# Gates of 128 tokens put by indirect 4-byte DMAs, one-hots made in two VectorE operations, in a decoder block with a product-key expert layer

## What is computed

```python
q = (xt @ wq).reshape(t, PEER_HEADS, 2, PEER_HALF_DIM)          # 8 heads, 2 halves
sc = jnp.einsum('thpc,hpnc->thpn', q, sub_keys)                  # 128 keys a half
top_v, top_i = lax.top_k(sc, PEER_TOPK)                          # 16 of each half
cand_v = top_v[..., 0, :, None] + top_v[..., 1, None, :]         # 256 candidate pairs
best_v, best_pos = lax.top_k(cand_v, PEER_TOPK)                  # 16 experts a head
expert = take(top_i[0] * 128 + top_i[1], best_pos)               # of 128 * 128
gate = jax.nn.softmax(best_v, axis=-1)
hc = jnp.einsum('cd,chkd->chk', xc, u[ec])
ac = gate * jax.nn.gelu(hc)
out = jnp.einsum('chk,chkd->cd', ac, v[ec])
```

## Time and profile before

| | before |
|---|---|
| median of 3 runs | 3343.63 us (3340.43 to 3347.16) |
| the profiled execution | 3340.54 us, span 3338.7 us |
| busy, share of the span: PE | 3216.9 us, 96% |
| PEld | 2994.6 us, 90% |
| DVE | 2480.9 us, 74% |
| ACT | 1111.0 us, 33% |
| POOL | 535.9 us, 16% |

### The profile page before, as it was taken

The page is one execution under the profiler, slowest core; times in us unless marked ns, Lnnn a source line. Parts: engine busy times, 40 slices in busy tenths (PEclk is TensorE's granted clock), DMA queues, the critical chain, the costliest instruction groups (busy, mean ns, idle before and its releaser), DMA issues.

```text
span 3338.7 us, 48188 instructions
## 1 busy us (share of the span) xinstructions
PE 3216.9 (96%) x17333; PEld 2994.6 (90%) x17333; DVE 2480.9 (74%) x3744; ACT 1111.0 (33%) x1411; POOL 535.9 (16%) x381
## 2 busy tenths in 40 slices
PE   7999999999988889999999999999999999999997
PEld 5777788898888779999999999999999999999785
DVE  6444434699979977878888887888888888885644
ACT  4224423222225543333333323333233333333432
POOL 2120000011143221111212111121211112110200
PEclk8999999999999999999999999999999999999998
DMA  3231122333356667878878787887878878773222
GB/s 139 86 126 47 54 88 96 110 110 110 110 184 223 236 242 269 295 281 285 300 274 298 270 293 281 283 302 266 298 273 286 291 278 303 272 250 120 97 93 101
DMA packets 230385, 694.37 MB, mean 208 GB/s; under 512 B 17328, under 2 KB 75184, under 8 KB 194864
## 3 DMA queue, kind: packets, MB, share of 16 engines
q1 hardware_dynamic: 188848, 418.77, 36.5%
q0 software_dynamic: 36864, 268.45, 22.6%
q10 hardware_dynamic: 4608, 6.29, 0.5%
HBM read 657.79 MB, written 35.65 MB: 208 GB/s over the span
## 4 chain that ended last, share of the span: by engine, by line
PE 62%; issue 18%; DVE 12%; DMA 5%; ACT 2%; POOL 1%; DVEq 1%; SPq 0%; POOLq 0%; ACTq 0%
PE bank L475 19%; PE bank L476 19%; PE bank L477 19%; DVE one_g L1521 3%; DMA raw<-in_u_t 3%; DVE w_lo L1191 2%; DMA raw<-in_v 1%; DVE row L1497 1%; ACT w_hi L865 1%; POOL picked L1755 1%; PE bank L567 1%; PE bank L568 1%; PE bank L590 1%; DVE one_j L1524 1%; DVE x_lo L1629 1%
## 5 line engine op out<-in xcount | busy, mean ns | idle before, releaser
L475 PE MATMUL bank<-x_hi,w_hi 128*128 128x384 f32 (+1 forms) x3024 | 1081.9, 358 | 36.2 <-DVE x_lo L1208 16.1
L476 PE MATMUL bank<-x_lo,w_hi 128*128 128x384 f32 (+1 forms) x3024 | 1070.3, 354 | 0.0
L477 PE MATMUL bank<-x_hi,w_lo 128*128 128x384 f32 (+1 forms) x3024 | 1070.1, 354 | 0.0
L865 ACT ACTIVATE w_hi<-raw 128x1024 fp32r<-128x1024 f32 (+1 forms) x668 | 689.2, 1049 | 909.0 <-DMA raw<-in_v 336.2
L1191 DVE TENSOR_TENSOR w_lo<-raw,w_hi 128x1024 fp32r<-128x1024 f32 (+1 forms) x638 | 766.5, 1218 | 201.7 <-ACT w_hi L865 192.6
L475 PE MATMUL bank<-a_hi,w_hi 128*128 128x384 f32 x2048 | 688.1, 336 | 14.3 <-DVE w_lo L1191 10.9
L476 PE MATMUL bank<-a_lo,w_hi 128*128 128x384 f32 x2048 | 685.7, 335 | 0.0
L477 PE MATMUL bank<-a_hi,w_lo 128*128 128x384 f32 x2048 | 685.6, 335 | 0.0
L475 PEld LDWEIGHTS bank<-x_hi,w_hi 128*128 128x128 f32 x3024 | 571.7, 189 | 87.1 <-DVE w_lo L1191 21.9
L477 PEld LDWEIGHTS bank<-x_hi,w_lo 128*128 128x128 f32 x3024 | 571.4, 189 | 39.2
L476 PEld LDWEIGHTS bank<-x_lo,w_hi 128*128 128x128 f32 x3024 | 572.0, 189 | 38.6 <-issue 1.2
(11 more groups left out here) (194 smaller groups left out, 2183.0 us busy)
## 6 DMA issues: line engine op xcount, KB each, us to landing
raw<-in_u_t SPq DMA_DIRECT2D x256, 512.0 KB
raw<-in_v SPq DMA_DIRECT2D x256, 512.0 KB
gate_matrix<-g_blk SPq DMA_DIRECT2D x12, 2048.0 KB, 10.7
g_tile<-gate_matrix SPq DMA_DIRECT2D x32, 768.0 KB, 10.5
raw<-in_w_o SPq DMA_DIRECT2D x32, 512.0 KB
raw<-in_w_q SPq DMA_DIRECT2D x32, 512.0 KB
raw<-in_w_gate SPq DMA_DIRECT2D x32, 512.0 KB
raw<-in_w_in SPq DMA_DIRECT2D x26, 512.0 KB
```

What stands on the lines that cost most here:

```text
L475: pe.matmul(out, w_hi[slot][:, blk, :], m_hi, start=first, stop=False)
L476: pe.matmul(out, w_hi[slot][:, blk, :], m_lo, start=False, stop=False)
L477: return pe.matmul(out, w_lo[slot][:, blk, :], m_hi, start=False, stop=last)
L865: act.activation(w_hi[slot][:, 8 * s:8 * s + n, :], raw[s][:, 0:n, :], ACT.Copy)\
```

## The change

The tokens whose gates go through one-hots are the last 256 of the 384; blocks of one-hots fall from 12 to 8 (ONE_TB). The gates of the first 128 tokens (PUT_TB = 4 blocks) are written directly into `gate_matrix` in DRAM: SP first stores zeros there during the attention heads (from `zeros`, which lies where `x_rows` is later), VectorE computes for each head the flat position `cell` and the value `put_gate`, and GpSimd issues one indirect DMA for each (head, k) that adds 128 elements of four bytes, one for each token. One head's puts wait until those of the head before have landed. ScalarE waits for all puts ahead of the first block, SP ahead of the first gate load.

The `picked` product moves from GpSimd to VectorE, and `expert` is computed head by head; `topk_step` counts 22. The plain spilled units rise from 7 to 11 and get all their `w_lo` on VectorE; the first five of those splits stand within and right behind the last head's top-k. The sixteen early row dots are now eight ahead of the blocks and eight within. In `one_hots` the keys i and j are compared in one operation into `one_ij`, and a second one multiplies the i part by the gate into `one_g`.

The diff, cut to its core:

```diff
-ALONE = 7
-ALONE_POOL = 3
+ALONE = 11
+PUT_TB = P // TB
+ONE_TB = N_TB - PUT_TB
-EARLY = ALONE - ALONE_POOL + N_TB
+EARLY = 16
...
@@ SP @@
-            with sp.Fori(2, HEADS) as n:
+            sp.wait_ge(zeros_made, 1)
+            for n in range(2, HEADS):
                 load_unit(n + U_HEAD, head_w(n))
+                if n - 2 < 2 * PUT_TB:
+                    b, half = divmod(n - 2, 2)
+                    sp.dma_start(g_dram[b, :, 64 * half:64 * half + 64, :],
+                                 zeros[:, :].rearrange("p (i t) -> p i t", t=TB)).then_inc(zeros_stored, 16)
...
+            sp.wait_ge(gates_put, 16 * TOPK * PH)
             sp.wait_ge(spill_stored, 16 * N_GROUPS)
...
@@ TensorE @@
-            for e in range(1, ALONE_POOL + 1):
+            for e in range(1, 6):
                 alone(e)
...
-                for t in range(TCD):
+                for t in range(1, TCD):
                     mm = pe.transpose(bank[i][:, t * P:(t + 1) * P],
...
-            for e in range(ALONE_POOL + 1, ALONE):
+            for e in range(6, ALONE):
                 alone(e)
...
@@ ScalarE @@
-                if e == ALONE_POOL - 1:
+                if e == 3:
                     gates(PH - 1)
                 spill(2 * (PH - 1) + e, e % 2, U_ALONE + e)
-                if e == ALONE_POOL:
+                if e == 5:
...
+            act.wait_ge(gates_put, 16 * TOPK * PH)
             for s in range(2):
                 g_block(s, s)
...
@@ VectorE, keys_and_gates @@
+                dve.wait_ge(pick_ready, 2 * hd + 2)
+                for p in range(2):
+                    ins = dve.tensor_tensor(
+                        picked[p][:, :, :].rearrange("p (t k) m -> p t k m", t=TC),
+                        pick[p][:, :, :].rearrange("p (t k) m -> p t k m", t=TC),
+                        t_if[p][:, :, :].unsqueeze(2).to_broadcast([P, TC, TOPK, TOPK]), ALU.mult)
+                step(ins)
...
+                dve.tensor_tensor(of_head(put_gate), b_exp[:, 0, :], b_inv[:, 0:1].to_broadcast([P, TOPK]), ALU.mult)
...
-                dve.wait_ge(picked_ready, 2 * hd + 2)
...
+                dve.scalar_tensor_tensor(of_head(expert), i_of[:, TCD, :], float(NK), j_of[:, TCD, :], ALU.mult, ALU.add)
+                dve.scalar_tensor_tensor(pair_e[:, 0, :], j_of[:, 0, :], float(NK * TB),
+                                         rope_c[:, 2:3].to_broadcast([P, TOPK]), ALU.mult, ALU.add)
+                step(dve.tensor_scalar(pair_e[:, 1, :], i_of[:, 0, :], float(TB), None, ALU.mult))
+                step(dve.tensor_tensor(of_head(cell), pair_e[:, 0, :], pair_e[:, 1, :], ALU.add))
...
@@ VectorE, the last head, the row dots and the one-hots @@
+            lo(U_ALONE + 1, (U_ALONE + 1) % 2)
             half_topk(step, 2 * PH - 2, 0)
+            lo(U_ALONE + 2, U_ALONE % 2)
             half_topk(step, 2 * PH - 1, 1)
+            lo(U_ALONE + 3, (U_ALONE + 1) % 2)
             best_pairs(step)
+            lo(U_ALONE + 4, U_ALONE % 2)
             keys_and_gates(step, PH - 1)
...
+            lo(U_ALONE + 5, (U_ALONE + 1) % 2)
...
+            for k in range(ALONE - 5):
+                lo(U_ALONE + 6 + k, (U_ALONE + k) % 2)
                 row_dot(k, k % 2, row_loads(k))
-            row_dot(3, 1, row_loads(3))
+            for k in range(ALONE - 5, EARLY - ONE_TB):
+                row_dot(k, k % 2, row_loads(k))
...
-                for t in range(OH):
-                    ins = dve.tensor_scalar(one_g[s][:, t, :], iota[:, :], column(hk_t[0], q * OH + t),
-                                            column(hk_t[2], q * OH + t), ALU.is_equal, ALU.mult)
-                ins.then_inc(oh_g, 1)
-                dve.tensor_tensor(one_j[s][:, :, :], iota[:, None, :].to_broadcast(o),
-                                  hk_t[1][:, bass.ds(OH * q, OH)].unsqueeze(2).to_broadcast(o), ALU.is_equal)\
-                   .then_inc(oh_j, 1)
+                dve.tensor_tensor(one_ij[s][:, :, :, :], iota[:, None, None, :].to_broadcast(o),
+                                  hk_t[:, 0:2, bass.ds(OH * q + P, OH)].unsqueeze(3).to_broadcast(o), ALU.is_equal)\
+                   .then_inc(oh_ij, 1)
+                dve.wait_ge(oh_ij, q + 1)
+                dve.tensor_tensor(one_g[s][:, :, :], one_ij[s][:, 0, :, :],
+                                  hk_t[:, 2, bass.ds(OH * q + P, OH)].unsqueeze(2).to_broadcast([P, OH, NK]), ALU.mult)\
+                   .then_inc(oh_g, 1)
...
@@ GpSimd @@
+            pool.memset(zeros[:, :], 0.0).then_inc(zeros_made, 1)
...
+            def put_gates(hd, rows=None):
+
+                pool.wait_ge(topk_step, PER_TOPK * (hd + 1))
+                if hd:
+                    pool.wait_ge(gates_put, 16 * TOPK * hd)
+                for k in range(TOPK):
+                    if rows is not None and k % 4 == 0 and k:
+                        load_row(rows + k // 4 - 1)
+                    pool.indirect_dma_start(g_dram.rearrange("b j i t -> (b j i t)").unsqueeze(1),
+                                            bass.IndirectOffsetOnAxis(ap=cell[:, hd, k:k + 1], axis=0),
+                                            put_gate[:, hd, k:k + 1], None, compute_op=ALU.add)\
+                        .then_inc(gates_put, 16)
...
+            pool.wait_ge(zeros_stored, 16 * 2 * PUT_TB)
+            for hd in range(PH - 1):
+                put_gates(hd)
+            pool.wait_ge(topk_step, PER_TOPK * PH)
+            pool.wait_ge(rows_out, 4)
+            for k in range(2):
+                load_row(k)
+            put_gates(PH - 1, rows=2)
+            for k in range(5, EARLY - ONE_TB + 1):
+                load_row(k)
+            for b in range(ONE_TB):
+                if b and b + EARLY - ONE_TB < EARLY:
+                    load_row(b + EARLY - ONE_TB)
                 block_lo(U_BLOCK + 1 + b)
```

More of the change, by code:

```diff
@@ L119, in build_block @@
         x_rows = at("x_rows", rest + 7 * K, [P, D])
-        expert = at("expert", rest + 15 * K, [P, ROWS], U32)
+        zeros = x_rows
+        expert = at("expert", rest + 15 * K, [P, PH, TOPK], U32)
         gate_rows = at("gate_rows", rest + 15 * K + 512, [P, ROWS])
@@ L161, in build_block @@
         sel = [at(f"sel{i}", one + (42 + 2 * i) * K, [P, TC, PH, TOPK]) for i in range(3)]
+        pair_e = at("pair_e", one + 59 * K, [P, 2, TOPK])
+        cell = at("cell", one + 59 * K + 512, [P, PH, TOPK], U32)
+        put_gate = at("put_gate", one + 60 * K, [P, PH, TOPK])
         t_v = [at(f"t_v{i}", one + 48 * K + 256 * i, [P, TC, TOPK]) for i in range(2)]
@@ L170, in build_block @@
         t_if = [at(f"t_if{i}", one + 53 * K + 256 * i, [P, TC, TOPK]) for i in range(2)]
-        hk_t = [at(f"hk_t{i}", one + 2 * K * i, [P, TD]) for i in range(3)]
-        one_g = [at(f"one_g{i}", one + (14 + 4 * i) * K, [P, OH, NK]) for i in range(2)]
-        one_j = [at(f"one_j{i}", one + (22 + 4 * i) * K, [P, OH, NK]) for i in range(2)]
+        hk_t = at("hk_t", one, [P, 3, TD])
+        one_ij = [at(f"one_ij{i}", one + (6 + 8 * i) * K, [P, 2, OH, NK]) for i in range(2)]
+        one_g = [at(f"one_g{i}", one + (22 + 4 * i) * K, [P, OH, NK]) for i in range(2)]
         g_blk = [at(f"g_blk{i}", one + (30 + 16 * i) * K, [P, NK, TB]) for i in range(2)]
@@ L755, in g_group @@
                         o = 4 * half + t
-                        mm = pe.matmul(out[:, t * P:(t + 1) * P], one_j[s][:, o, :], one_g[s][:, o, :],
+                        mm = pe.matmul(out[:, t * P:(t + 1) * P], one_ij[s][:, 1, o, :], one_g[s][:, o, :],
                                        start=True, stop=True)
@@ L1785, in load_row @@
                 pool.indirect_dma_start(row[b][:, :], None, u_rows if k < ROWS else v,
-                                        bass.IndirectOffsetOnAxis(ap=expert[:, k % ROWS:k % ROWS + 1], axis=0))\
+                                        bass.IndirectOffsetOnAxis(ap=expert[:, k % ROWS // TOPK, k % TOPK:k % TOPK + 1], axis=0))\
                     .then_inc(row_in[b], 16)
-            pool.wait_ge(expert_ready, 1)
-            pool.wait_ge(rows_out, 4)
-            for k in range(6):
-                load_row(k)
             def block_lo(u):
@@ L1800, in block_lo @@
                         .then_inc(lo_ready, 1)
[L1802 to L1804 removed]
+            pool.wait_ge(zeros_stored, 16 * 2 * PUT_TB)
[11 more added lines that the diff above has]
+                    load_row(b + EARLY - ONE_TB)
                 block_lo(U_BLOCK + 1 + b)
             for s in range(2):
[L1807 removed]
+                pool.wait_ge(g_stored[s], 16 * (ONE_TB // 2))
             for k in range(EARLY, 2 * ROWS):
```

95 lines of the change are left out of this document (35 added, 60 removed).

## The result

The kernel after takes 3308.11 us (median; 3305.56 to 3311.9), the kernel before, run beside it, 3345.39 us (3340.43 to 3348.09): a ratio of 0.9893, with a 95% interval from 0.9878 to 0.9908. The profiled executions have spans of 3338.7 and 3308.0 us, 30.7 apart.

A forecast was written before the change was run, and what follows sets the result against it. TensorE was taken to bound the top-k heads (41.63 us each), VectorE the gate-matrix stage. Terms -43.3 + 9.9 + 0 - 2.7 + 8.3 + 0.5 = -27.3 us, from 3343.6, gave 3316 us; own range 3308 to 3328, with rivals 3286 to 3345.

The forecast's parts named there:

- Four blocks for four units: Gate-matrix stage: four blocks fewer save 76.6 us, four more plain spilled units cost 33.3 us; net -43.3 us.
- Two-operation one-hots: Blocks on VectorE: 20.4 us each instead of 19.16, with two stalls of 2.2 us; +9.9 us over eight blocks.
- Rival A: Blocks: GpSimd's subtractions no longer stall the one-hots, 16.0 us a block; 3281 to 3300 us, chance 0.15.
- The heads: Top-k heads: VectorE changes by -0.85 to +0.25 us a head, TensorE still sets 41.63; 0, at most +1 us in all.
- heads still 41.6 apart: Sign expected in the profile after: the top-k heads keep their period of 41.6 us.
- The tail: Last head's top-k: last cell at 960.7 us, TensorE waits about 1.9 and 3.0 us before units 4 and 5; -2.7 us.
- The entry: Entry to the blocks: row 7's gather waits for dot 5, one-hots start at A + 19.4 instead of A + 11.1; +8.3 us.
- part 6: Puts on GpSimd: 1.25 us to twice that each, within a head; weight loads perhaps slowed, 0 to +6 us, 0.5 counted.
- near 1 us each: Sign expected in the profile after: puts on GpSimd take near 1 us each.
- Rival B: DMA engines: slow puts hold up the first block, gain gone from 0.23 us a packet; 3455 us at 327 ns, chance 0.12.
- Rival C: Heads turn VectorE-bound, short operations delayed while puts are written, 7 us a head; +38 us, 3354 us, chance 0.06.
- Rival D: Gain lost in small parts: late row 7 gather, loads held up in each head, memset or store; +22, 3338 us, chance 0.12.

The follow-up runs named there:

- e3: Kernel after with w_lo's subtractions in its eight blocks moved from GpSimd to VectorE: 3294.69 us, ratio 0.9855 to the kernel before.
- e5: Kernel after with the scalar one-hots of the kernel before in its eight blocks: 3303.81 us, ratio 0.9878 to the kernel before.
- e2: Kernel before with only the two picked products moved from GpSimd to VectorE: 3332.01 us, ratio 0.9969 to the kernel before.
- e1: Kernel after without its 128 puts and the waits for them: 3307.29 us, ratio 0.9894 to the kernel before.
- e6: e5 with w_lo's subtractions in the blocks on VectorE as well: 3294.83 us, ratio 0.9857 to the kernel before.
- e7: Kernel before with w_lo's subtractions in its twelve blocks moved from GpSimd to VectorE: 3323.31 us, ratio 0.9933 to the kernel before.
- e9: e6 with rows 6 and 7 gathered into free buffers, gathers placed among the last puts: 3290.80 us, ratio 0.9843 to the kernel before.
- e10: e6 with four further MEMSETs on VectorE at the entry of the expert groups: 3291.46 us, ratio 0.9834 to the kernel before.
- e11: Kernel after with four further MEMSETs on VectorE at the entry of the expert groups: 3318.33 us, ratio 0.9918 to the kernel before.

## Why the prediction was right, and where it was not

The forecast was 3316 us, 27.6 less than before; it is 3308.1, and 37 less than the kernel before beside it. The profiles differ by 30.7 us, against a sum of 27.3. The sum's own range, 3308 to 3328, redone from its terms begins at 3310, so 3308.1 lies just below it and within the stated 3286 to 3345.

The near hit is partly luck, since errors in both directions offset each other. The profiles, both cut at the same points, give:

| part | forecast, us | measured, us |
|---|---|---|
| heads, to the last spill | 0 | -4.2 |
| last top-k and plain units, to the start of the last | 33.3 - 2.7 = +30.6 | +27.4 |
| from there to the first one-hots | +8.3 | +12.3 |
| the blocks | -76.6 + 9.9 = -66.7 | -65.0 |
| loads slowed by puts | +0.5 | not seen |
| ahead of the first spill, and behind the blocks | 0 | -1.2 |

1. Four blocks for four units: right. A plain unit takes 8.32 us (998.55 to 1006.87), and the stage lasts 164.9 us for eight blocks against 229.9 for twelve.

2. Two-operation one-hots: right. A block takes 20.6 us against the 20.4 forecast, with stalls of 2.08 (e3) against the 2.2 taken. Rival A, no stall, is out. e5 shows the price by itself: the older form makes a block 19.17, so the new one costs 8 x 1.4 = 11.5 us where the sum had +9.9. It is a loss, not a gain, for all its fewer instructions.

3. The heads: the step failed. It read TensorE's pace, 41.63 us, off two heads near the end, where TensorE was 272.2 of 274 us busy, and counted VectorE's gain as slack. The first heads of the same trace ran at 40.4, while VectorE was at 41.6 in all of them. e2 shows that the later ones were held back by VectorE's way through GpSimd, and that moving the product is worth 10.4 us in the kernel before. VectorE's own gain was forecast rightly (-0.85 to +0.25 us a head): its heads are 40.9 us apart after, still 0.6 more than TensorE's, which TensorE's lead covers. In the comparison with after, the seven spills from 645.28 to 890.52 become those from 644.21 to 886.19: the heads give 4.2 us by the last spill (912.10 to 906.80) where 0 was counted. The step's "0, at most +1 us" left out a gain because a TensorE that was 99% busy was taken for the one that set the pace. The sign "heads still 41.6 apart" failed with it.

4. The tail: right for VectorE, low for TensorE. The last `cell` comes at 954.3 us; 960.7 less the 5.3 us by which the last spill came earlier is 955.4. The five small operations cost 0.16 to 0.18 us each. TensorE waits 3.1 us in its plain units where 1.9 and 3.0 were forecast, and the transposes lose the stretch at half clock that followed the wait of 7.3 us before: nine of 0.42 us there, six of 0.27 now. In all the stretch gives 5.8 us instead of 2.7.

5. The entry: direction right, size off. The one-hots begin 23.4 us after the start of the last plain unit (998.55 to 1021.98), not 19.4, and TensorE waits 16.7, not 12. The step followed dot 5 behind the last `lo` and took row 5 to be there. But row 5's own gather is queued behind puts: its buffer was free when dot 3 ended (992.3 us), the gather was issued at 1001.82, behind the gather of row 4 and the last four puts, and the row landed 8.58 us late for the dot. e1 puts the whole at 5.1 us. A price of 1.25 for a put, the lower end, was in part 6, but it was held only against a head's length and not against the gathers it stands among; the pitch of a put is 1.85.

6. The puts: right. They cost nothing in the heads (e1), and the last of them was issued at 999.0 us, 29 us before the first eviction, for which ScalarE waited only for TensorE. On GpSimd they took 1.55 us and 0.30 to the next, so 1.85 between the bounds of 1.25 and 2.5; the sign "near 1 us each" failed, since they took half as long again. Rival B is out: a packet takes 49 ns, below its nearest row of 58 and far below the 210 from which it would decide.

7. Rival C is out. VectorE's busy time in the heads is the same with 97 puts as without (261.42 and 261.43 us), so issuing the puts delays none of VectorE's operations to a measurable degree. The other way round it shows: a put is 1.55 at the median and 1.77 on average (226.7 us for 128), 2.60 at most. Of the 43 puts over 1.6 us, 36 began while VectorE ran an operation with two tensor inputs (`w_lo`, `cand`, `pick`, `picked`, a row dot), of the 85 others 7. The Trainium skill, page "SBUF — State Buffer", section "Who interferes with whom", has the lock work both ways; of the two only GpSimd's side is borne out here. For the subtractions the trace agrees with its rule: each stretches VectorE's work by 2.08 us.

Rival D, losses in small parts, did not come true for the change itself: the expert groups take 1848.3 us against 1849.4, and the one loss of size is the entry. In the kernels built on it, what is won ahead of the expert groups is in part gone at their end (e6 enters them 24.9 us before after, and ends them 12.8 before it).

## What to carry to other kernels

An engine that is 99% busy over a window can still be led by another one: compare its period early and late in the loop with the period of the others, and ask what the 1% was waiting for. When GpSimd gets many short DMAs, count them against the gathers that share its queue, not only against the length of the loop. Moving GpSimd's SBUF arithmetic to a VectorE that is the bound paid in all three kernels that isolate it (e2, e3, e7). In the blocks GpSimd's 2.4 us had stalled VectorE for 2.1 while the same work costs VectorE 1.13; in the heads VectorE had waited for the result as well. The fastest kernels here, e9 and e10, do both this and the scalar one-hots, and are 0.5 and 0.6% faster than the kernel after. A forecast that adds up terms stage by stage can hit by offsetting errors; check each term, not the sum.

## What the runs showed of the hardware

- An indirect DMA that adds occupies GpSimd for 1.55 us for 128 elements, one that only writes or reads for 0.95 to 0.96 us, with 0.30 between them. It has 144 packets where the plain write has 32, and a packet takes 49 instead of 11 ns.
- Puts do not lengthen VectorE's operations (261.42 against 261.43 us busy), while single puts are lengthened up to 2.60 us, 36 of 43 of them when they began under a VectorE operation with two tensor inputs.
- After a wait of 7.3 us TensorE's granted clock was 0.50 from 955 to 960 us of the kernel before, and a transpose took 0.42 us; without that wait it took 0.27.
- Stretching by GpSimd's subtraction is the same, 2.1 us, for scalar pieces of 128 elements, for products with two inputs in SBUF and for comparisons of 2048 elements.
- The expert groups, with the same matmuls of 334 ns, took 1847.1 to 1860.4 us in one execution each of kernels whose edits lie ahead of them or at their entry. A delay of 9.0 us at the entry made one kernel (e10) no slower and the other (e11) slower by 8 us (ratio 0.9918 against 0.9893). The cause is open.
